# Moving the modulation-weight loads ahead by two blocks in the DMA queue of a two-layer hybrid backbone step

## What is computed

```python
mod = silu(cond) @ ada_w + ada_b                       # 1024 -> 6*1024, once for c_ctx and once for c
sh1, sc1, g1, sh2, sc2, g2 = split(mod, 6)
h = rms_norm(x, norm1_g) * (1 + sc1) + sh1
u = h @ w_in                                           # 1024 -> 3304 columns
y = concat(ssd(u_ssd), rwkv(u_rwkv), mlstm(u_ml)) @ w_out
x = x + g1 * y
h = rms_norm(x, norm2_g) * (1 + sc2) + sh2
x = x + g2 * ((silu(h @ ffn_w1) * (h @ ffn_w3)) @ ffn_w2)
```

## Time and profile before

| | |
|---|---|
| Runs (median of 3) | 2348.7 us (2347.61 to 2369.55) |
| Profiled execution, its own time | 2348.7 us |
| Profiled execution, span of the trace | 2347.0 us |
| PE busy | 2127.3 us, 91% of the span |
| Chain of work that ended last: share on PE | 83% |
| Mean granted TensorE clock | 0.97 of full speed |
| DMA of the SP queue | 163.59 MB, 23.4% of the 16 engines' span |

### The profile page before, as it was taken

How to read it: one execution, slowest core, us unless ns; L and a number is a source line. 1 busy time by engine, 2 the same in 40 slices (tenths; PEclk the granted TensorE clock), 3 DMA queues, 4 the chain that set the end, 5 groups by cost and what they waited for, 6 DMA issues and landing times.

```text
span 2347.0 us, 46026 instructions
## 1 busy us (share of the span) xinstructions
PE 2127.3 (91%) x20570; PEld 1957.8 (83%) x20570; DVE 804.4 (34%) x1363; ACT 764.6 (33%) x1352; POOL 731.3 (31%) x539
## 2 busy tenths in 40 slices
PE   4999999888779999999979989988879799999996
PEld 3998766777779999999869986667758799999986
DVE  4755265454430111010148453654551311101003
ACT  3535453333242222221154354433332422222111
POOL 4332162234113333332223223432413233333221
PEclk8999999999889999999989999999989899999998
DMA  7453201000112222243226431010002122222221
GB/s 246 145 169 111 60 8 37 5 3 2 37 38 80 75 78 72 75 127 130 75 85 197 132 103 21 2 40 3 3 1 72 46 74 80 72 74 76 65 65 55
DMA packets 260498, 166.67 MB, mean 71 GB/s; under 512 B 29939, under 2 KB 234229, under 8 KB 260301
## 3 DMA queue, kind: packets, MB, share of 16 engines
q1 hardware_dynamic: 259846, 163.59, 23.4%
q10 hardware_dynamic: 454, 0.14, 0.0%
HBM read 159.59 MB, written 4.12 MB: 70 GB/s over the span
## 4 chain that ended last, share of the span: by engine, by line
PE 83%; DVE 8%; ACT 5%; issue 3%; POOL 1%; another core or an unknown queue 0%; DVEq 0%; ACTq 0%; POOLq 0%
PE PS L890 20%; PE PS L892 20%; PE PS L891 20%; PE PS L1279 4%; PE PS L841 2%; PE PS L854 2%; DVE arena L1942 1%; DVE arena L1934 1%; PE PS L1424 1%; PE PS L951 1%; PE PS L1345 1%; PE PS L1297 1%; PE PS L1108 1%; PE PS L1145 1%; PE PS L1159 1%
## 5 line engine op out<-in xcount | busy, mean ns | idle before, releaser
L890 PE MATMUL PS<-rwp_r,whi_r 128*128 128x320 f32 x2880 | 906.1, 315 | 62.1 <-DVE arena_r L1946 35.9
L892 PE MATMUL PS<-rwp_r,ring_r 128*128 128x320 f32 x2880 | 895.4, 311 | 0.0
L803 POOL TENSOR_TENSOR ring_r<-ring,whi_r 128x1024 fp32r<-128x1024 f32 (+1 forms) x204 | 496.6, 2436 | 1191.1 <-ACT whi_r L1612 1191.1
L891 PE MATMUL PS<-arena_r,whi_r 128*128 128x320 f32 x2240 | 696.3, 311 | 0.0
L890 PEld LDWEIGHTS PS<-rwp_r,whi_r 128*128 128x128 f32 x2880 | 546.3, 190 | 79.7 <-issue 51.4
L892 PEld LDWEIGHTS PS<-rwp_r,ring_r 128*128 128x128 f32 x2880 | 545.9, 190 | 0.0
L891 PEld LDWEIGHTS PS<-arena_r,whi_r 128*128 128x128 f32 x2240 | 424.6, 190 | 0.0
L1612 ACT ACTIVATE whi_r<-ring 128x1024 fp32r<-128x1024 f32 (+1 forms) x204 | 211.4, 1039 | 587.8 <-PE PS L892 587.7
L891 PE MATMUL PS<-U_r,whi_r 128*128 128x320 f32 x960 | 298.1, 311 | 0.0
L2481 DVE TENSOR_TENSOR U<-arena,PS 128x640 f32<-128x640 f32 x44 | 36.1, 821 | 555.0 <-PE PS L892 555.0
L2460 DVE SCALAR_TENSOR_TENSOR x<-PS,MOD,x 128x128 f32<-128x128 f32 (+2 forms) x96 | 36.1, 434 | 429.3 <-PE PS L892 429.3
(11 more groups left out here) (372 smaller groups left out, 2629.9 us busy)
## 6 DMA issues: line engine op xcount, KB each, us to landing
ring<-in_ffn_w SPq DMA_DIRECT2D x120, 512.0 KB, 3.8
rwp<-in_ada_w SPq DMA_DIRECT2D x64, 512.0 KB, 4.8
ring<-in_w_in SPq DMA_DIRECT2D x50, 512.0 KB, 4.7
U<-in_ada_w SPq DMA_DIRECT2D x16, 512.0 KB, 10.3
ring<-in_w_out SPq DMA_DIRECT2D x16, 512.0 KB, 4.5
arena<-in_ada_w SPq DMA_DIRECT2D x16, 512.0 KB, 4.9
ring<-in_ffn_w SPq DMA_DIRECT2D x16, 384.0 KB, 3.4
out<-U SPq DMA_DIRECT2D x5, 512.0 KB, 2.7
```

The lines of the kernel that those rows point to most:

```text
L803: g.tensor_tensor(rings_r[:, slot_of[n], 0:size(n), :], slot(n)[:, 0:size(n), :], whis[:, q_ % 2, 0:size(n), :].bitcast(F32), ALU.subtract ...
L890: mm(out, w[0][:, k, :], hi[:, cols], start=start, stop=False)
L891: mm(out, w[0][:, k, :], lo[:, cols], start=False, stop=False)
L892: return mm(out, w[1][:, k, :], hi[:, cols], start=False, stop=stop)
```

## The change

The units of step n are put right behind `w_in` block n in the list, for every n, instead of behind block n + 2. No load is added or removed, and no instruction of PE, ACT, DVE or POOL is changed. Only the order of SP's queue is different: `w_in` 1, the two units of step 1, `w_in` 2, the two units of step 2, `w_in` 3, and so on to `w_in` 24, the unit of step 24, `w_in` 25.

```diff
             for n, m in enumerate(ORDER):
                 if lay or n > 1:
                     BLOCKS.append((lay, "w_in", m))
-
-                if n > 1:
-                    BLOCKS += [(lay, "ada_w", g, u) for g, u in ADA_AFTER[n - 2]]
-            BLOCKS += [(lay, "ada_w", g, u) for n in (NU - 2, NU - 1) for g, u in ADA_AFTER[n]]
+                BLOCKS += [(lay, "ada_w", g, u) for g, u in ADA_AFTER[n]]
             BLOCKS += [(lay, "w_out", m) for m in range(KT)]
```

## The result

The changed kernel takes 2387.8 us (median of 4 runs, 2381.6 to 2398.1) against 2355.9 us before (4 runs, 2347.6 to 2369.6) in the same comparison: ratio 1.0132, 95% interval 1.0092 to 1.0172. The forecast was 2363 us in a range of 2352 to 2380. The profiled execution took 2379.2 us, with a span of 2377.4 us, 30.4 us more than before's.

The account below looks back on a forecast made before the run. PE was taken to bound the kernel, busy 91% of the span; late w_in blocks cost 7.2 us in each of two layers, +14.4 us on 2348.7, giving 2363 us, range 2352 to 2380.

Parts of the forecast that it names:

- no gain in the units: Projection: ada_w units still wait for one of two slots, so they come no earlier where needed; gain 0.
- the deadline: Steps 3 to 9: w_in block ready 10.36 us after b(n), but a step takes 8.25 to 8.37, so PE waits.
- The recurrence: Step-by-step times b(n) at which PE can begin step n+1, ending at b(9) = 148.15 against 140.95: 7.2 us a layer.
- the 7.3 us row: Profile row with one w_in landing of 7.3 us, against the 6.05 us the sum used.
- the bounds: Other landing times in the recurrence: 5.3 us gives about +8 in all, 7.3 gives +24, 7.7 about +28.
- all that was costed at nothing: rows_out, rows_in, small_loads, DVE, layer 1's start and steps after 9: shifted or delayed, cost 0.
- the second rival: Each of six new PE gaps per layer lowers the clock, costing 1.7 us: +35 us in all, 2384 us; chance 0.07.
- longer landings: Rival: w_in landings in the projection take longer than 6.05 us, +18 to +31 us, 2367 to 2380; chance 0.14.
- the base: Starting time of the sum: the profiled execution's 2348.7 us, also the median of the runs.

Follow-up runs that it names:

- one_unit_ordered: Units of steps 10 to 24 right behind their own w_in block, step 9's one block later, steps 1 to 8 as in the kernel before: ratio 0.9998.
- filled_gaps: Changed kernel plus five unused matmuls behind the units of each of steps 2 to 8, closing nearly all PE gaps: ratio 1.0066 to before.
- between: Changed kernel, but in two-unit steps the w_in block of step n+1 goes between the two units of step n: ratio 1.0051 to before.
- same_delay_busy: Kernel before plus 35 unused matmuls at the end of step 8 of each layer, delaying PE without idling: ratio 1.0063.
- copy_first: Changed kernel with ACT's copy for the pick moved ahead of the split in steps 2 to 8: ratio 1.0110 to before.

## Why the prediction was wrong, point by point

**Right: no gain in the units.** Units are issued 0.3 us before PE begins a step, at 82.65 and 82.88 us, and the waits of PE had none for them before or after.

**Right: the deadline and its size.** The recurrence gave 7.2 us for a layer and +14.4 us in all; the delay at the full clock is +16.9 us. In the profiled execution the waits are 8.2 us in layer 0 and 7.8 in layer 1. They come nearly where the text put them: in layer 0 at the splits of the steps 4 and 6 to 9 and at the picks of the steps 3 and 5 (forecast: the splits of 4 to 9 and the pick of 3, with that of 5 only 0.1 us from deciding). Step 5 began without a wait, at 105.14 us, since step 4 before it ran in part at 1.2 GHz. The sum was low by two terms. The landing was taken as 6.05 us from the earlier trace rows, and the blocks of layer 0 took 6.1 to 7.0; and POOL's split of block 4 took 2.97 us instead of 2.44. The last block, with 7.0 us, made the 2.16 us wait where 1.2 was forecast. It stands behind the units of step 8, as the block of the 7.3 us row does (125:131), which the working left for the bounds. Those (+8 to +24) held the sum. In layer 1 there was one wait more than forecast, 0.8 us for the split of block 10.

**Right: all that was costed at nothing.** `rows_out` is issued at 257.97 us (with the forecast's 244.5 and 13 us of delay, 257.5), and one_unit_ordered has the time of before. DVE, `small_loads` and the start of layer 1 left no new wait. One reading was wrong without effect: the block issued at 83.80 us before the change is used at 108.2 us, 24 us and three steps later, not 33 us and four.

**Wrong: the clock.** The step that failed is the second rival, "the clock falls in the new gaps", which was left out of the sum and given 0.07. It was argued away by one row, the gap of 2.27 us at 72.7 us that left the clock at 1.00. The changed kernel lost the clock in layer 0 at a pair of 0.96 and 1.48 us and after a wait of 2.16, and in layer 1 at a pair of 0.71 and 0.89, while 2.27 us in front of step 2 went free in both kernels. One gap that had gone free was no bound on sixteen others, and the gaps were weighed one by one, though the forecast's own list has such a pair (0.85 us at the pick of step 3, then 1.14 at the split of step 4). The rival's price for each stretch (1.7 us) came from a good row, but not every gap was followed by one: 13 us over all runs, and 6.8 in the profiled execution, not 20. That its +35 us came near the measured 31 is in part luck. With both terms at their measured size and a base of 2357 us, the same sum gives 2357 + 17 + 13 = 2387 us. The rule of the Trainium skill that was weighed there (Perfetto Trace Analysis, Matmul Optimizations: matmuls belong back to back, because power scales with use) spoke for this, and filled_gaps agrees with it: the same delay costs 12 us less with PE kept busy. The trace of between does not: 9 us of waits, none over 1.5 us, left the clock of both projections at 1.00.

**Wrong: the base.** The sum was made on the profiled execution of before, 2348.7 us, which is also near the fastest: over 61 later executions the medians are 2356 to 2362 us. The three runs shown (2347.6, 2348.7 and 2369.6) had that spread in them, and their median happened to be low. With a base of 2357 the same working gives 2371. That alone would not have reached the measured 2388. With that base the range would have reached to 2388 as well, but its upper part stood for longer landings, and the clock had no part in it.

**Open.** That the clock's part of the loss comes from idling is settled (filled_gaps and same_delay_busy), and the traces show its places. What is open is why the wait in front of step 2 goes free, and which pairs of waits do. The places were read in one execution of each kernel, and stretches at 1.2 GHz also come and go in later stages, for every kernel, before the change too.

## What to carry to other kernels

Before moving a load ahead in a shared queue, count for each load behind it how many steps it is issued ahead of its use, with all waits that stand before it; here two steps were free and one cost 17 us, because a block was ready 9.7 to 11.0 us after its issue and a step takes 8.3. Price the waits of a TensorE that otherwise runs without a break one by one, with the pairs among them, and not by one row that went free: here 16 us of them brought 13 us of lower clock, in the traces all of it behind the few that were long or close together, and 9 us of waits of at most 1.4 us cost no more than the measurement can tell (3.5 ± 2.8). And split a difference into span x clock and span x (1 - clock) before explaining it: over 21 runs of the changed kernel the first had a standard deviation of 2.2 us, the second one of 7.7.

## What the runs showed of the hardware

- The length of a matmul right behind a wait doesn't tell whether the clock falls. In copy_first 2.22 us was followed by a matmul of 0.64 us and 1.81 us by one of 0.42, and both by 3.4 us at 1.2 GHz. Nor does the length of the wait alone: 2.27 us in front of step 2 went free in every trace that has it. In the kernel between, five waits of 0.2 to 1.4 us in each projection, one to a step at most, left the clock at 1.00:

```profile
75.00:150.00 75.00, 69.82 (x657) 67.03 (x657) 58.77 (x88) 34.91 (x47) 27.64 (x19) 1.00 0.58 178
1232.00:1315.00 83.00, 79.02 (x729) 75.84 (x730) 63.95 (x103) 38.38 (x51) 24.79 (x10) 1.00 0.59 180
```

- A load with one unit ahead landed later when another unit was issued right behind it: median 5.4 us (up to 7.0) in between, against 4.4 us (up to 5.3) where nothing followed at once. The two are from different steps, so that the unit behind is the reason is not shown.
- PE waited 16.0 us more in the two projections and lost 16.9 us at the full clock: nothing of it was won back later. PE has 78% of the chain of work that ended last.
